# A three-block transformer kernel on one core: SBUF tiles placed so that every matmul operand tile begins on a multiple of 128 bytes

## The reference

```python
def first_block(x, ...):                       # 2 layers
    for l in range(DEPTH):
        y = _mla(x, ...) if l < n_a else _swa(x, ..., k_band, v_band, rel_bias)
        x = _layernorm(alpha * x + y, ln_mix_g[l], ln_mix_b[l])
        x = _layernorm(alpha * x + _mlp(x, mlp_w_up[l], mlp_w_down[l]), ln_mlp_g[l], ln_mlp_b[l])
    return x

def _mlp(x, w_up, w_down):                     # 1024 -> 4096 -> 1024
    h = jax.nn.relu(x @ w_up)
    return (h * h) @ w_down

def second_block(x, p, ...):                   # 1 layer
    z = rmsnorm(x, g_mix) @ w_in
    zb, zc, zx, zq, zk, zv = jnp.split(z, ...)
    y_c = zb * causal_dwconv3(zc * zx, conv_w, conv_b)
    y_a = dilated_attention(q, k, v)           # q, k: rmsnorm of zq, zk by heads
    x = x + jnp.concatenate([rmsnorm(y_c, ...), rmsnorm(y_a, ...)], axis=-1) @ w_out
    h = rmsnorm(x, g_ffn)
    gate = causal_dwconv3(h @ w_gate, ffn_conv_w, ffn_conv_b)
    x = x + (jax.nn.silu(gate) * (h @ w_up)) @ w_down      # 1024 -> 2816 -> 1024
    ple_gate = jax.nn.sigmoid(rmsnorm(x, g_ple) @ w_ple_gate)
    return x + ple_gate * (p @ w_ple_proj)
```

## Time and profile before

| | us |
|---|---|
| median of 3 runs | 1812.21 (1811.75 to 1813.03) |
| the profiled execution, its own time | 1814.21 |
| its span, from the first instruction to the last | 1812.4 |
| TensorE (PE) busy in the span | 1773.6 (98%) |
| VectorE (DVE) busy | 983.6 (54%) |
| ScalarE (ACT) busy | 668.3 (37%) |
| mean granted TensorE clock | 0.992 |

### The profile page before, as it was taken

One profiled execution on the slowest core, in us unless ns is written; L12 is line 12 of the kernel. 1 busy time (PEld: TensorE's weight loads), 2 busy tenths in 40 slices (PEclk: granted clock), 3 DMA queues, 4 the chain that ended last, 5 costly groups with the idle time before them and its releaser, 6 DMA issues.

```text
span 1812.4 us, 23486 instructions
## 1 busy us (share of the span) xinstructions
PE 1773.6 (98%) x9636; PEld 1510.2 (83%) x9636; DVE 983.6 (54%) x1433; ACT 668.3 (37%) x938; POOL 1.9 (0%) x11
## 2 busy tenths in 40 slices
PE   9999999999999999999999999999998999999998
PEld 7777998888889988998888889888787788888886
DVE  3666663334347666753434347657566665356554
ACT  3445442313134576441313233434354232222332
POOL 0000000000000000000000000000000000000000
PEclk9899999999999999999999999999999999999999
DMA  8211232222322221223222223112111223322341
GB/s 283 93 52 42 94 117 93 93 96 90 116 85 101 72 71 66 76 81 105 93 93 94 91 97 113 55 62 93 47 71 58 94 103 122 122 93 93 116 151 59
DMA packets 28597, 169.74 MB, mean 94 GB/s; under 512 B 2848, under 2 KB 7392, under 8 KB 9440
## 3 DMA queue, kind: packets, MB, share of 16 engines
q1 hardware_dynamic: 22592, 156.44, 24.2%
q10 hardware_dynamic: 5920, 12.08, 2.0%
HBM read 166.39 MB, written 5.27 MB: 95 GB/s over the span
## 4 chain that ended last, share of the span: by engine, by line
PE 89%; DVE 5%; ACT 4%; issue 1%; DMA 1%; DVEq 0%; SPq 0%; ACTq 0%
PE ps L1664 29%; PE ps L1666 27%; PE ps L1665 27%; DVE w_lo L888 2%; PE ps L1797 2%; ACT w_hi L419 1%; DMA stage<-slabs 1%; PE ps L1776 1%; PE ps L2010 0%; ACT y L576 0%; PE ps L2142 0%; PE ps L1737 0%; ACT act_hi L581 0%; PE ps L1917 0%; PE ps L1728 0%
## 5 line engine op out<-in xcount | busy, mean ns | idle before, releaser
L1664 PE MATMUL ps<-act_hi,w_lo 128*128 128x512 f32 (+1 forms) x1504 | 545.9, 363 | 14.6 <-issue 4.4
L1666 PE MATMUL ps<-act_lo,w_hi 128*128 128x512 f32 (+1 forms) x1504 | 538.7, 358 | 0.0
L1665 PE MATMUL ps<-act_hi,w_hi 128*128 128x512 f32 (+1 forms) x1504 | 538.7, 358 | 0.0
L419 ACT ACTIVATE w_hi<-stage 128x2048 fp32r<-128x2048 f32 (+4 forms) x147 | 267.5, 1820 | 378.4 <-PE ps L1666 377.2
L888 DVE TENSOR_TENSOR w_lo<-stage,w_hi 128x2048 fp32r<-128x2048 f32 (+6 forms) x152 | 322.5, 2123 | 85.8 <-ACT w_hi L419 78.9
L1664 PEld LDWEIGHTS ps<-act_hi,w_lo 128*128 128x128 f32 x1504 | 284.4, 189 | 62.5 <-issue 13.8
L1666 PEld LDWEIGHTS ps<-act_lo,w_hi 128*128 128x128 f32 x1504 | 284.3, 189 | 42.3
L1665 PEld LDWEIGHTS ps<-act_hi,w_hi 128*128 128x128 f32 x1504 | 284.4, 189 | 40.1
L1664 PE MATMUL ps<-hid_hi,w_lo 128*128 128x512 f32 (+1 forms) x608 | 218.4, 359 | 2.1 <-DVE w_lo L888 2.1
L1666 PE MATMUL ps<-hid_lo,w_hi 128*128 128x512 f32 (+1 forms) x608 | 216.9, 357 | 0.0
L1665 PE MATMUL ps<-hid_hi,w_hi 128*128 128x512 f32 (+1 forms) x608 | 215.3, 354 | 0.0
(11 more groups left out here) (293 smaller groups left out, 2172.2 us busy)
## 6 DMA issues: line engine op xcount, KB each, us to landing
stage<-slabs SPq DMA_DIRECT2D x147, 1024.0 KB, 4.8
bias_rows<-bias_line ACTq DMA_DIRECT2D x1, 3072.0 KB, 15.2
strips<-dilated ACTq DMA_DIRECT2D x2, 1024.0 KB, 4.8
out<-y ACTq DMA_DIRECT2D x4, 512.0 KB, 2.6
y<-x_t ACTq DMA_DIRECT2D x3, 512.0 KB, 8.8
strips<-bias_rows ACTq DMA_DIRECT2D x1, 1024.0 KB, 5.6
strips<-bias_rows ACTq DMA_DIRECT2D x2, 512.0 KB, 4.2
stage<-slabs SPq DMA_DIRECT2D x3, 256.0 KB, 8.6
```

The costliest lines, as they stand in the source:

```text
L419: nc.scalar.activation(w_hi[p][:, 0:w], stage[s][:, 0:w], ACT.Copy).then_inc(cast_hi, 1)
L1664: mm(out, l_lo, r_hi, start=start, stop=False, skip_group_check=shared)
L1665: mm(out, l_hi, r_hi, start=False, stop=False, skip_group_check=shared)
L1666: return mm(out, l_hi, r_lo, start=False, stop=stop, skip_group_check=shared)
```

## The change

The tiles are allocated in another order, so that every tile that a matmul reads begins on a multiple of 128 bytes. The small tiles go behind the large ones, `negsink` is widened from 16 to 32 columns so that the shared area behind it begins at 135,680 (a multiple of 128, and of 512), `u_pad` and `gate` go behind the tiles that they had shifted, and `top` is rounded up before `p_raw`. No instruction is added, removed or moved on any engine, and no operand changes its shape or its offset inside its tile; the addresses alone differ. Exceptions to the multiple of 128 are columns of small tiles (`tok_r`, `rden`) that a few matmuls load one column at a time; they stay as they are.

```diff
+LINE_BYTES = 128
...
         tmp = keep("tmp", [P, 2, 2, T])
-        vec = keep("vec", [P, NVEC])
         mat = keep("mat", [P, 4, P])
         ident, ones, ones64, swap = (mat[:, i, :] for i in range(4))
-        eps = keep("eps", [P, 2])
         sum1 = keep("sum1", [P, T])
         sum2 = keep("sum2", [P, T])
         rstd = keep("rstd", [P, T])
         stat = keep("stat", [P, T])
-        tok_v, tok_s, tok_r, tok_q = (keep(f"tok_{x}", [P, 16]) for x in "vsrq")
-        rstd_tok = keep("rstd_tok", [P, 4])
-        table_mark = keep("table_mark", [P, 1])
-        mark = keep("mark", [P, 1])
         negmax = keep("negmax", [P, 4 * 16])
         rowsum = keep("rowsum", [P, 4 * 16])
         sinkexp = keep("sinkexp", [P, 4 * 16])
         rden = keep("rden", [P, 4 * 16])
-        negsink = keep("negsink", [P, 16])
+        tok_v, tok_s, tok_r, tok_q = (keep(f"tok_{x}", [P, 16]) for x in "vsrq")
+        vec = keep("vec", [P, NVEC])
+        rstd_tok = keep("rstd_tok", [P, 4])
+        eps = keep("eps", [P, 2])
+        table_mark = keep("table_mark", [P, 1])
+        mark = keep("mark", [P, 1])
+
+        negsink = keep("negsink", [P, 32])
...
-        u_pad, d_prob, d_pt_hi, d_pt_lo, rstd2, _ = part(
-            top, ("u_pad", [P, 2, T + 2], F32), ("d_prob", [P, 2, CAUSAL.total], F32),
-            ("d_pt_hi", [P, CAUSAL.total], F32R), ("d_pt_lo", [P, CAUSAL.total], F32R), ("rstd2", [P, T], F32))
+        d_prob, d_pt_hi, d_pt_lo, rstd2, u_pad, _ = part(
+            top, ("d_prob", [P, 2, CAUSAL.total], F32), ("d_pt_hi", [P, CAUSAL.total], F32R),
+            ("d_pt_lo", [P, CAUSAL.total], F32R), ("rstd2", [P, T], F32), ("u_pad", [P, 2, T + 2], F32))
...
-        gate, gconv, silu, ffh, top = part(
-            top, ("gate", [P, 2, T + 2], F32), ("gconv", [P, 2, T], F32), ("silu", [P, 2, T], F32),
-            ("ffh", [P, 2, T], F32))
+        gconv, silu, ffh, gate, top = part(
+            top, ("gconv", [P, 2, T], F32), ("silu", [P, 2, T], F32), ("ffh", [P, 2, T], F32),
+            ("gate", [P, 2, T + 2], F32))
+        top += -top % (LINE_BYTES // 4)
...
-            nc.vector.tensor_scalar(negsink[:, :], vec[:, VEC["sink"]:VEC["sink"] + 16], -1.0, None, ALU.mult)
+            nc.vector.tensor_scalar(negsink[:, 0:16], vec[:, VEC["sink"]:VEC["sink"] + 16], -1.0, None, ALU.mult)
```

## The result

| | median, us | runs | ratio to before |
|---|---|---|---|
| kernel before | 1811.98 (1811.41 to 1813.03) | 6 | |
| kernel after | 1822.21 (1820.14 to 1823.91) | 6 | 1.0056 [1.0045, 1.0066] |

The change made the kernel 10.2 us slower. The forecast was 1809.8 us with a range of 1804.0 to 1814.0, so both the sign and the range were wrong. The time fell where rival D had it, 1815.4 to 1825.8. The profiled execution of after took 1823.67 us with a span of 1821.9, against 1814.21 and 1812.4 before.

The account below looks back on a forecast made before the run. It took TensorE, busy 98% of the span, as the bound, so only matmul pace could move: -5.6 (512 columns) + 3.2 (256 columns) + 0 (attention) = -2.4 us, from 1812.2 to 1809.8 us, range 1804.0 to 1814.0.

Parts of the forecast that it names:

- rival D: 512-column matmuls of `hid`, `h`, `o`, `c`: 128 apart is bad, halves go to 120.0 ns; 1815.4 to 1825.8 us; chance 0.12.
- 0/0 rows: Trace rows whose moving and stationary tiles both start at 0 modulo 128 bytes: 226.7 ns at 512 columns, 120.0 at 256.
- `hid`, -3.0 us: 26 slabs of `hid` at 512 columns go from 10.98 to 10.88 us each, with boundaries a gain of 3.0 us.
- `h`, -1.2: 528 matmuls of `h` at 512 columns gain 2.2 ns each, 1.2 us.
- `o` and `c`, -0.8: At 512 columns, 240 `o` and 156 `c` matmuls gain 2.2 ns each, 0.5 and 0.3 us.
- Value slabs, -0.3: The two value slabs of MLA, 48 matmuls at 512 columns, gain 6.8 ns each, 0.3 us.
- `p`, -0.3: 48 matmuls of `p` at 512 columns gain 6.9 ns each, 0.3 us.
- Halves, +3.2: 256-column matmuls of `act` on the third buffer, `hid` and `o` on buffers 0 and 1 slow to 120.0 ns, losing 3.2 us.
- VectorE and the other engines, nothing: VectorE subtraction stays at 1225 ns; ScalarE, DMAs and the wider `negsink` add nothing beside 98% TensorE.
- Attention, 0: Attention scores and mixes: taken as 0, between a gain of 0.5 us and a loss of 0.9.
- Clock, 1.7 to either side: Stretches at half clock after attention waits: a shift may add or spare one, 1.7 us, counted only in the range.
- Rival C: All large products: pace belongs to what runs then, not to the offset, so nothing changes; 1812.2 us; chance 0.14.

Follow-up runs that it names:

- e1: Kernel after with `negsink` 64 columns wide, shared area 128 bytes later, at distance 0 modulo 256 from weight buffers 0 and 1: 1807.36 us, ratio 0.997.
- e5: Kernel after with `negsink` 128 columns wide, shared area 384 bytes later, `hid` and `h` 256 bytes from the weights modulo 512: 1810.33 us, one run.
- e3: Kernel after with `negsink` 48 columns wide, shared area 64 bytes later, `hid` and `h` 192 bytes ahead of the weights modulo 256: 1818.69 us, one run.
- e2: Kernel after with `negsink` 64 columns wide and a 128-byte tile in front, so `act`, weights and shared area begin on multiples of 256: 1805.46 us, one run.
- e8: Kernel after with `negsink` 64 columns wide and `w_lo` of buffers 0 and 1 moved 64 bytes further: 1832.1 us, one run.
- e4: Kernel after with `negsink` 72 columns wide, shared area 160 bytes later, `hid` and `h` 32 bytes ahead of the weights: 1823.62 us, one run.

## Why the prediction was wrong

**The step that failed** is the choice of the class: "offset" was taken modulo 128, and every product that the change brings to 0/0 was given the pace of the 0/0 rows. In the kernel before, all of these rows are 0 apart modulo 256, while the change brings `hid`, `h`, `o` and `c` to 128. The prediction names this as its weak point, and set it aside because two rows at ±64 agree, "as they would if the pattern repeats every 128 bytes". That inference was one pair of rows at 256 columns, put to use at 512. At 512 columns its own rows spoke against it: `hid`, 64/0, and the value slab, 0/64, are the same distance modulo 128, and they had 228.8 and 233.5 ns. The runs show a period of 256 (e1 against after, and e5 against e1) and that ±64 differ at 512 columns (e3). D, given 0.12, was what happened.

**Term by term.**
- `hid`, -3.0 us: 233.3 ns instead of 226.7. In the first MLP the running difference rises by 2.6 us between 259 and 544, and in all the term is about +5.5 (26 slabs by 11.20 - 10.99).
- `h`, -1.2: 232.5 and, in the second stretch, 233.3 ns. The running difference rises by 0.9 in the first stretch, from 1505 to 1583, and by 1.0 in the second, which begins behind `p`; +1.9.
- `o` and `c`, -0.8: `o` costs 0.4 between 1303 and 1505 instead, and `c`, the value slabs and the halves from 78 to 259 us cost 0.3 together.
- Value slabs, -0.3: they went from 233.5 to 232.2 ns, nearly nothing; 128 replaced 192.
- `p`, -0.3: right, and by luck. The area moved it by 64 and the new place of `gate` with the rounding of `top` by 96, which took it from 96 to 256, that is 0; rounding to 128 did not ensure that. It runs at 226.6 ns.
- Halves, +3.2: the direction was right, the size not. They went to 118.5 and a little over instead of 120.0, so `act` on the third buffer and `hid` on buffer 0 cost 0.8 ns each and not 2.3 and 2.1; `o` on buffer 1 cost 5.3 and not 6.8. e1, where they do lie 0 apart, shows the 120.0.
- VectorE and the other engines, nothing: right, 1225 and 1226 ns.
- Attention, 0: nearly right. Between 617.87 and 719.75 of before it cost 0.4 us, and in the second attention, from the half-clock stretch to 1303, it gave 0.1 back. No experiment took it apart.
- Clock, 1.7 to either side: the new stretch at 1164 cost about that. The first 78 us were 1.2 faster, with 6.8 us at half clock instead of 13.7 in before; but e5 and e2, with 6.8 too, were 0.3 slower and 3.1 faster than before there. So that start is not shown to be the clock's, and nothing of it was in the sum.

**Rival C.** The pace did change with the addresses alone: with the same instructions in the same order, `hid` ran at 226.7, 229.0 or 233.3 ns, as the distance was 0, 64, or 128 and 192. C had on its side the Trainium skill, page SBUF — State Buffer, section "Who interferes with whom", by which the moving read and the weight load have ports of their own and are independent. The runs disagree as to the pace; whether the one read waits for the other no run shows.

**D's own working** had the right place and the right pace (the 233.6 of `p` for 2172 matmuls). It gave 1825.8 at that pace in part because it also took the halves at 120.0. Its threshold, a gain of 1.4 ns each, sets the 3.2 us of the halves against the 2172 alone; with the 1.0 us of `p`, the value slabs and the boundaries, which it keeps, it would be 1.0 ns.

**What stays open.** Why the distance matters is not shown: no run looks into the memory. At 256 columns 64 and 192 each show two paces, 113 and 118 ns, and nothing here tells what chooses between them. The first 78 us differ by up to 3.4 us between these profiles, with no cause shown, and most experiments are one run; their argument is the paces, not the times. What decides whether a half-clock stretch falls behind a wait was not settled either: it came and went between kernels whose matmuls before it had shifted by a few us.

## What to carry to other kernels

When a change moves addresses, write down for each pair of operands what the pair's distance becomes, and look whether the trace has a row with that very distance before taking a pace for it; a period that two rows suggest is a guess until a third row stands on it, and it has to be held against every row at hand, of the other width too. Here, placing the moving tiles a multiple of 256 bytes from their weights was worth 0.3% and two lines, while rounding every start to 128, which left them 128 apart, cost 0.6%. Gains of some us in a kernel at 98% TensorE have to be read slab by slab, since stretches at half clock, up to 1.7 us for each 3.4, came and went among these kernels and are as large as the terms themselves. In a wait they cost less: e1 has 6.8 us of them at 1370 where before has 3.4, with TensorE busy for 1.0 of the first 3.4, and the table shows no loss there.

## What the runs showed of the hardware that was not expected

- The pace of a 512-column matmul with its weight load, in these kernels, depends on the distance of its two operands modulo 256 bytes: 226.7 ns at 0, 229 to 230 at 64, 232.2 to 234.2 at the other distances measured, 64 behind among them.
- At 256 columns the order is reversed: distance 0 is the slowest, 120.0 ns, and 113.2 is to be had at 64.
- Where only one of the two weight tiles lies badly, one gap in three is the slowest (235.8 against 228.3 and 229.2 ns in e8), the other two are slower than 226.7 as well, and the average, 231.1, is still worse than 64 apart for both.
- Two half-clock stretches near 1303 and 1323, 3.0 us in all, are in the profiles of before, at 1311 and 1332 of after, and at 1308 and 1329 of e4, and absent in those of all others but e8, which has half-clock stretches at 1300 and 1314.
